# A mixture-of-experts trunk on one core: the scatter of an expert's rows moved behind the first products of the next expert

## The reference, cut to what matters

```python
logits = xn @ w_router
top_val, top_idx = top_k(logits, 2);  gates = softmax(top_val) at top_idx, 0 elsewhere
for e in range(8):                       # D=1024, D_FF_EXPERT=3584
    hg = xn @ w_gate[e];  hu = xn @ w_up[e]
    hh = silu(hg) * hu * gates[:, e]
    h  = h + hh @ w_down[e]
return rmsnorm(h, g_final)
```

## Time and profile before

| what | value |
|---|---|
| median of three runs | 1386.95 us |
| the profiled execution, its own time | 1392.87 us |
| its span | 1391.1 us |
| its mean granted TensorE clock | 0.952 |
| PE busy | 1251.6 us, 90% of the span |
| DMA moved | 413.83 MB, mean 297 GB/s |

### The profile page before, as it was taken

One profiled execution on the slowest core, in us unless ns is written; L12 is line 12 of the kernel. 1 busy time (PEld: TensorE's weight loads), 2 busy tenths in 40 slices (PEclk: granted clock), 3 DMA queues, 4 the chain that ended last, 5 costly groups with the idle time before them and its releaser, 6 DMA issues.

```text
span 1391.1 us, 20342 instructions
## 1 busy us (share of the span) xinstructions
PE 1251.6 (90%) x8591; PEld 639.3 (46%) x8592; DVE 334.6 (24%) x741; ACT 267.5 (19%) x490; POOL 28.2 (2%) x43
## 2 busy tenths in 40 slices
PE   6999999999998898999788987899969888799997
PEld 4765777787664533444332332334433233233443
DVE  2354666676343300110010010020001001002002
ACT  2232333332261010111110110111111011011111
POOL 2100000000100100000000000000000000000000
PEclk9979999999999799999989999999998999999999
DMA  9511744347333299999979999999997999999991
GB/s 341 174 53 32 272 170 164 104 171 261 131 122 127 103 376 400 389 393 396 390 275 394 397 390 393 400 389 393 397 388 296 394 397 390 395 399 390 393 398 63
DMA packets 173127, 413.83 MB, mean 297 GB/s; under 512 B 4166, under 2 KB 9404, under 8 KB 172780
## 3 DMA queue, kind: packets, MB, share of 16 engines
q1 hardware_dynamic: 171660, 409.58, 78.8%
q0 software_dynamic: 1088, 1.81, 0.4%
q10 hardware_dynamic: 288, 1.05, 0.2%
HBM read 411.38 MB, written 1.05 MB: 296 GB/s over the span
## 4 chain that ended last, share of the span: by engine, by line
PE 81%; DMA 8%; issue 6%; DVE 4%; ACT 2%; SPq 0%; POOL 0%; POOLq 0%; ACTq 0%; DVEq 0%
PE ps L1302 16%; PE ps L1280 16%; PE ps L1284 8%; DMA ring<-in_moe_w_up 7%; PE ps L1345 6%; PE ps L1041 4%; PE ps L1037 4%; PE ps L1038 4%; PE ps L1317 3%; PE ps L1273 3%; PE ps L1022 2%; PE ps L1213 2%; PE ps L1161 2%; PE ps L1330 1%; PE ps L908 1%
## 5 line engine op out<-in xcount | busy, mean ns | idle before, releaser
L1302 PE MATMUL ps<-ring,arena 128*64 128x512 f32 x560 | 265.6, 632 | 54.8 <-DMA ring<-in_moe_w_up 27.8
L1303 PE MATMUL ps<-ring,arena 128*64 128x512 f32 x560 | 265.9, 632 | 0.0
L1280 PE MATMUL ps<-ring,arena 128*32 128x512 f32 x1512 | 261.9, 593 | 1.4 <-issue 1.4
L1281 PE MATMUL ps<-ring,arena 128*32 128x512 f32 x504 | 258.0, 594 | 0.0
L1302 PEld LDWEIGHTS ps<-ring,arena 128*64 128x64 f32 x560 | 79.1, 145 | 229.9 <-issue 193.8
L1284 PE MATMUL ps<-ring,arena 128*32 128x256 f32 x2016 | 155.4, 379 | 0.0
L1284 PEld LDWEIGHTS ps<-ring,arena 128*32 128x32 f32 x2016 | 66.5, 110 | 149.8 <-issue 149.8
L1346 PE MATMUL ps<-ring,arena 128*64 128x512 f32 x280 | 126.6, 598 | 0.0
L1345 PE MATMUL ps<-ring,arena 128*64 128x512 f32 x280 | 126.6, 598 | 0.0
L1784 DVE TENSOR_TENSOR arena<-arena 64x512 f32<-64x512 f32 x35 | 24.7, 707 | 382.7 <-ACT arena L830 382.7
L1556 DVE TENSOR_TENSOR w_lo<-ring,w_hi 128x2048 fp32r<-128x2048 f32 x33 | 75.6, 2292 | 60.2 <-ACT w_hi L727 58.7
(11 more groups left out here) (276 smaller groups left out, 1381.0 us busy)
## 6 DMA issues: line engine op xcount, KB each, us to landing
ring<-in_moe_w_up SPq DMA_DIRECT2D x56, 2048.0 KB, 21.3
ring<-in_moe_w_down SPq DMA_DIRECT2D x56, 2048.0 KB, 19.5
ring<-in_moe_w_gate SPq DMA_DIRECT2D x55, 2048.0 KB, 19.5
ring<-in_ffn_w_gate SPq DMA_DIRECT2D x5, 2048.0 KB, 7.9
ring<-in_ffn_w_up SPq DMA_DIRECT2D x5, 2048.0 KB, 7.9
ring<-in_ffn_w_down SPq DMA_DIRECT2D x5, 2048.0 KB, 7.8
ring<-in_mla_w_o SPq DMA_DIRECT2D x2, 2048.0 KB, 23.8
ring<-in_swa_w_q SPq DMA_DIRECT2D x2, 2048.0 KB, 8.4
```

The source lines that it names most:

```text
L1280: pe.matmul(ps[32 * j:32 * j + 32, bank, :], thirds[j], left, start=first, stop=last)
L1281: pe.matmul(ps[SLOTS:P, bank, :], thirds[2], right, start=first, stop=last)
L1302: pe.matmul(ps[0:NARROW, 2 * a, :], lhs, wg[:, k, :], start=(k == 0), stop=(k == KD - 1))
L1303: mm = pe.matmul(ps[64:64 + NARROW, 2 * a + 1, :], lhs, wu[:, k, :], start=(k == 0), stop=(k == KD - 1))
```

## The change

The scatter moves from the head of an item to behind products(0). Products of chunk 1 follow it, which write banks 2 and 3, so the fourth result of the scatter goes to bank 4, the bank of the transposes, in place of bank 2. Two waits change with it: products(1) no longer waits for the addition of the scatter's fourth result but, as all other chunks do, for `hh_ready`; and the scatter's fourth product waits until ACT has copied the last transposes of the item before out of bank 4. The first transposes of the new item, which overwrite bank 4, wait for hh of chunk 0, which DVE makes after its four additions.

```diff
-        SCATTER_BANK = (7, 5, 6, 2)
+        SCATTER_BANK = (7, 5, 6, 4)
@@ products
-                if c == 1:
-                    pe.wait_ge(s.h_added, i * 4 + 5)
-                else:
-                    pe.wait_ge(s.hh_ready, i * (2 * ECH) + (2 * max(c - 1, 0) + 1))
+                pe.wait_ge(s.hh_ready, i * (2 * ECH) + (2 * max(c - 1, 0) + 1))
@@ scatter
                     if j == 3:
-                        pe.wait_ge(s.xgT_ready_v, i + 2)
+                        pe.wait_ge(s.hhT_ready, i * ECH + 1)
@@ pe_item
             def pe_item(i, narrow):
-                scatter(i)
                 for c in range(ECH):
                     products(i, c, narrow)
+                    if c == 0:
+                        scatter(i)
                     if c == 4:
                         scatter_T(i)
```

## The result

The changed kernel is slower: 1400.42 us median (20 runs) against 1394.36 us of the kernel before beside it (20 runs), a ratio of 1.0039 with a 95% interval of 1.0023 to 1.0055, that is about 5.4 us by the ratio and 6.1 us by the medians. The forecast was a gain of 8.2 us. The kernel before itself came out 7 us above the 1386.95 us of its first three runs, on which the forecast stood; the ratio is what counts.

What follows compares the result with a forecast made beforehand. Narrow items were taken as bound by the weight stream, wide ones by PE. Two restarts of 3.67 us plus 0.84 us at item 1 gave 8.2 us, from 1386.95 to 1378.8 us; own range 1375 to 1383, wider range 1372 to 1387.

Steps and rivals of the forecast that it cites:

- What bounds the kernel: Expert loop: narrow items bound by the weight stream, wide ones by PE; stream stops at steps from wide to narrow.
- Scatter behind products(0) at items 2 and 5: At the stream's restarts after the pause, 3.67 us saved at each of two starts, 7.3 us; upper bound 12.9 us.
- The low clock: After the pause before items 2 and 5: stays where it is in time and falls on products(0) instead.
- hole opened before d1: After u3 at the restarts: no new stream hole, or one of at most half a microsecond; margin 0.1 us.
- The pauses themselves: Before items 2 and 5: stay at 13 us; a changed length would make the prediction wrong.
- The wait for ysb at items 1, 4 and 7: Narrow-to-wide steps: products(0) covers PE's 0.84 us idle; 0.84 us gained at item 1, nothing at items 4 and 7.
- The waits for u3: In items 4 and 7: PE, waiting 0.62 and 0.74 us before, would wait 1.4 to 1.6 us.
- Items 0, 3 and 6, the bank, the waits: No gain at these items; bank 4 and new waits cost nothing, hh(0) ready some 2.5 us after the last scatter product.
- The rivals: Three alternatives: more saved (1371.6 us, 0.12), restart not the limit (1386.1 us, 0.14), slower by a code load (0.04).
- the slow case that I gave, a further code load: Items 2 and 5: PE stalls again for code, a whole 12 us pause each, +16 us, 1402.8 us; chance 0.04.

Runs made afterwards that it cites:

- A shorter stream: Kernel before and changed kernel, each loading only a quarter of every down piece: 1310.26 and 1310.25 us, ratios 0.9387 and 0.9393 to the kernel before.
- the reverse: Against the kernel before, scatter behind products(0) in wide items only, at the head of narrow items: 1402.16 us, ratio 1.0055.

## Why the prediction was wrong, point by point

**What bounds the kernel: right.** Stream in narrow items, PE in wide ones, two holes at the steps from wide to narrow. A shorter stream left neither loss nor gain.

**Scatter behind products(0) at items 2 and 5: right, in size too.** Forecast 3.67 us each, measured 4.17 and 3.45; alone (wide items left as they were) 7 to 8 us in all by the timed runs, where the forecast had 7.3. The low clock did stay with the end of the pause and fell on the products. No hole opened before d1. The pauses themselves were 0.32 and 0.34 us longer, not the same, which the forecast had given as a sign of being wrong; they count against the wide items in the table.

**The wait for ysb at items 1, 4 and 7: the step that failed.** The forecast asked what the scatter waits for there (0.84 us, kept at item 1, nothing at 4 and 7) and when u3 comes, but not when u0 does, which the very first product after the move needs. The trace of before had what was needed: narrow items end on the stream, so the next item's first pieces are the last to arrive, and u0 of item 4 was issued at 889.29, some 25 us before its use. A scatter that runs while PE would otherwise wait costs nothing; moved behind the wait it costs its 3.67 us in the wide item, where PE is the limit, and a wait of 4.2 to 4.4 us was followed by the low clock each of the five times that the traces show one (in the two traces of the changed kernel and in that of the reverse): 2.9 us more at item 4. In place of -0.84, 0 and 0 us it was +4.04, +6.15 and +4.05 for the stretches around these items in the profile. How much of it is the displaced scatter and how much the clock changes from run to run (the second profile of the same kernel has 4.4 us less). The waits for u3 did not grow to 1.5 us, they vanished.

**Items 0, 3 and 6, the bank, the waits: right.** The bank and the waits cost nothing, as the run with them alone shows. Item 0 is 0.15 us longer, items 3 and 6 nothing: from g3 of item 2 and of item 5 to products(0) of items 4 and 7 the time is the same within 0.1 us (201.02 and 201.07; 200.97 and 200.91). DVE had hh of chunk 0 ready 2.2 us after the last scatter product at item 2 and 2.9 at item 4, the forecast had 2.5.

**The rivals.** The mechanism of the slow case that I gave, a further code load, was not what happened in the changed kernel: its pauses were 13.71 and 13.64 us and no product stopped. It did appear, small, once the bodies were put in another order. The case that came true, work that had been cover, was not among the rivals, and the range stopped at no change because of it. That the measured 1400.42 us lies near the 1402.8 of that slow case is chance: its mechanism did not occur, and 7.4 us of the number are the base that moved.

## What to carry to other kernels

Where the kernel waits in turn for a stream and for an engine, moving work needs two questions at each place: what does it delay where it stands, and what does it cover there. At a step out of a stream-bound stretch, work that needs nothing from the stream belongs ahead of the first product that does; at a restart of a dry stream it belongs behind the product that frees the slots. Here the two places lie in two bodies of one loop, and each body wants its own order: 7 to 8 us faster than before, in place of 3 to 6 us slower.

## What the runs showed of the hardware

A jump across a long body cost 13.2 to 13.7 us of PE under a full stream, 10.7 to 11.3 us under the shorter one, and 5.6 to 6.1 us when the order in the code was turned round. That order alone made the kernel 16.7 us faster by the medians (12.3 us in the trace of the loop), more than any place of the scatter: of the kernels here that load all the weights, those with the short body first are the fastest. The Trainium skill, "Runtime: NRT & Kernel Launch", section Instruction fetch mechanics, says that a taken branch whose target is not in the blocks at hand has to fetch it before execution goes on. The traces agree: three blocks in the pause of 13.39 us, one in that of 5.75 us.

The granted clock after a short idle is not fixed by the idle alone: 0.66 in the five microseconds after a wait of 2.56 us in one execution, 1.00 after waits of 2.29 and 2.60 us in another, 0.50 or 0.73 after 4.3 us. In the untouched attention part one execution was 8 us ahead of the eleven others, by a stretch at the full clock that the kernel before ran partly at the low one (0.89 and 0.86 in the windows), which is as much as the whole effect that was looked for; only a ruler laid on the part that was changed, or many timed runs, could see it.
